# A fourth split slot at each stage's start, and four jobs side by side at three feed-forward starts

## The reference, cut to what matters

```python
def swiglu(x, w_gu, w_down):
    gate, up = jnp.split(x @ w_gu, 2, axis=-1)
    return (jax.nn.silu(gate) * up) @ w_down
...
    y = swiglu(rmsnorm(h, ffn1_pre_g[l]), ffn1_w_gu[l], ffn1_w_down[l])
    h = h + 0.5 * rmsnorm(y, ffn1_post_g[l])
    u = rmsnorm(h, mix_pre_g[l])
    proj = u @ w_in[l]
...
    h = h + rmsnorm(merged @ w_out[l], mix_post_g[l])
```

## Time and profile before

| | us |
|---|---|
| median of 3 runs (lowest, highest) | 3282.03 (3281.15, 3282.69) |
| the profiled execution, its own time | 3282.84 |
| its span | 3281.0 |
| PE busy | 3251.3 (99%) |
| DVE busy | 2377.1 (72%) |
| ACT busy | 1695.7 (52%) |
| POOL busy | 320.3 (10%) |
| boundary 1 to 2: first job of stage 2 starts at | 872.20 |
| boundary 2 to 3: first job of stage 3 starts at | 1216.07 |

### The profile page before, as it was taken

The page is one execution under the profiler, slowest core; times in us unless marked ns, Lnnn a source line. Parts: engine busy times, 40 slices in busy tenths (PEclk is TensorE's granted clock), DMA queues, the critical chain, the costliest instruction groups (busy, mean ns, idle before and its releaser), DMA issues.

```text
span 3281.0 us, 51592 instructions
## 1 busy us (share of the span) xinstructions
PE 3251.3 (99%) x20356; PEld 2902.2 (88%) x20356; DVE 2377.1 (72%) x4254; ACT 1695.7 (52%) x3071; POOL 320.3 (10%) x289
## 2 busy tenths in 40 slices
PE   9999999999999999999999999999999999999998
PEld 7999888888899998999888888899988888889998
DVE  7877764766697768777755766787868676658776
ACT  5555553645465545555553654564547374336553
POOL 1000110121010001000201121000000001201000
PEclk9999999999999999999999999999999999999999
DMA  4333433352233332333424263233332322322332
GB/s 143 109 105 121 125 81 87 84 153 89 85 99 102 113 99 90 110 103 116 125 68 125 54 151 103 68 110 107 109 100 88 93 77 71 103 96 97 101 112 84
DMA packets 118562, 332.80 MB, mean 101 GB/s; under 512 B 18984, under 2 KB 21800, under 8 KB 118320
## 3 DMA queue, kind: packets, MB, share of 16 engines
q1 hardware_dynamic: 106352, 308.40, 30.1%
q0 software_dynamic: 11680, 20.56, 3.2%
q10 hardware_dynamic: 288, 0.52, 0.0%
HBM read 306.23 MB, written 4.21 MB: 95 GB/s over the span
## 4 chain that ended last, share of the span: by engine, by line
PE 91%; DVE 6%; ACT 1%; DMA 1%; issue 1%; SPq 0%; POOL 0%; DVEq 0%; ACTq 0%
PE PS L838 89%; PE PS L1242 2%; DVE acc L1969 1%; DVE wl L1940 1%; DVE h L2024 1%; DVE tmp L2021 1%; DVE ul L1977 1%; DMA raw<-in_win 0%; ACT wh L1361 0%; DVE stk L2433 0%; DMA tmp<-tmp 0%; ACT tmp L1361 0%; SPq L3034 0%; ACT stk L1361 0%; DVE lru L2766 0%
## 5 line engine op out<-in xcount | busy, mean ns | idle before, releaser
L1940 DVE TENSOR_TENSOR wl<-raw,wh 128x1024 fp32r<-128x1024 f32 (+2 forms) x615 | 632.8, 1032 | 253.2 <-ACT wh L1361 247.4
L1361 ACT ACTIVATE wh<-raw 128x1024 fp32r<-128x1024 f32 (+2 forms) x619 | 535.0, 870 | 353.7 <-PE PS L838 331.8
L838 PE MATMUL PS<-bh,wh 128*128 128x256 f32 x2520 | 696.2, 276 | 0.0
L838 PE MATMUL PS<-bh,wl 128*128 128x256 f32 x2520 | 696.2, 276 | 0.0
L838 PE MATMUL PS<-bl,wh 128*128 128x256 f32 x2520 | 695.9, 276 | 0.0
L838 PE MATMUL PS<-uh,wh 128*128 128x512 f32 (+2 forms) x1368 | 525.6, 384 | 7.7 <-DVE stkf L2568 2.7
L838 PE MATMUL PS<-ul,wh 128*128 128x512 f32 (+2 forms) x1368 | 517.7, 378 | 0.0
L838 PE MATMUL PS<-uh,wl 128*128 128x512 f32 (+2 forms) x1368 | 517.5, 378 | 0.0
L838 PEld LDWEIGHTS PS<-bh,wh 128*128 128x128 f32 x2520 | 473.1, 188 | 0.6
L838 PEld LDWEIGHTS PS<-bh,wl 128*128 128x128 f32 x2520 | 473.0, 188 | 0.6
L838 PEld LDWEIGHTS PS<-bl,wh 128*128 128x128 f32 x2520 | 473.1, 188 | 0.0
(11 more groups left out here) (280 smaller groups left out, 5819.7 us busy)
## 6 DMA issues: line engine op xcount, KB each, us to landing
raw<-in_gu SPq DMA_DIRECT2D x218, 512.0 KB, 3.3
raw<-in_win SPq DMA_DIRECT2D x139, 512.0 KB, 3.5
raw<-in_dn SPq DMA_DIRECT2D x80, 320.0 KB, 2.9
raw<-in_dn SPq DMA_DIRECT2D x40, 512.0 KB, 3.6
raw<-in_wbr SPq DMA_DIRECT2D x72, 256.0 KB, 2.7
raw<-in_wout SPq DMA_DIRECT2D x24, 512.0 KB, 3.2
raw<-in_dn SPq DMA_DIRECT2D x40, 256.0 KB, 2.7
raw<-in_wv SPq DMA_DIRECT2D x20, 512.0 KB, 3.4
```

What stands on the lines that cost most here:

```text
L838: return e.matmul(out, lhs, rhs, start=start, stop=stop, skip_group_check=True)
L1361: return e.activation(out, in_, f, scale=scale, **more)
L1940: tt(lo, src, hi, SUB).then_inc(*S.lo.up(("lo", c)))
```

## The change

There are four opener slots a stage instead of three; `oh` moves to a lower place in the same area so that both hold four. The fourth job's cut p0+3 is now split with the other openers, ahead of the held tiles, on ACT and on DVE. With the slot free, cuts p0+4 to p0+7 wait for the cuts eight before. In the feed-forwards v = 2, 3 and 5 `group_halves` takes four jobs, so each k of a half is 12 matmuls of 256 columns; `after` is p0+4 and `more` is p0+5, `sums_pre` comes behind 6 matmuls of `after` and `spread_pre` behind 18. In the mixers v = 1, 4 and 6 three jobs stay side by side, and p0+3 is still `after`. In `mixer_2` (v = 6) two memsets move, since the fourth slot's neighbours now lie on their tiles.

```diff
-        oh = sb("oh", [P, 3, 1088], F32R, where["X"] + 57600)
-        ol = sb("ol", [P, 3, 1088], F32R, where["X"] + 57600 + 3 * 4352)
+        oh = sb("oh", [P, 4, 1088], F32R, where["X"] + 32768)
+        ol = sb("ol", [P, 4, 1088], F32R, where["X"] + 57600)
...
-        OPENERS = {first_of(v) + i: i for v in range(1, 7) for i in range(3)}
+        OPENERS = {first_of(v) + i: i for v in range(1, 7) for i in range(4)}
...
+                at = (1, 3) if len(jobs) == 4 else (3, 5)
                 n = 0
-                for _ in dense(after, v, "u"):
-                    n += 1
-                    if n == 3:
-                        sums_pre(v)
-                n = 0
-                for _ in dense(more, v, "u"):
-                    n += 1
-                    if n == 1:
-                        spread_pre(v)
+                for job in (after, more):
+                    for _ in dense(job, v, "u"):
+                        n += 1
+                        if n == at[0]:
+                            sums_pre(v)
+                        elif n == at[1]:
+                            spread_pre(v)
 
             def ffn(v):
                 order = [JOBS[a, v, f] for f in range(PLAIN) for a in ("gate", "up")]
-                begin(v, order[:3], order[3], order[4])
-                for job in order[5:]:
+                n = 4 if 0 < v < 7 else 3
+                begin(v, order[:n], order[n], order[n + 1])
+                for job in order[n + 2:]:
                     run(job, v)
...
-                ahead(p0 + 2)
+                ahead(p0 + 3)
                 act(small[:, 48:49], eps, ACT.Sqrt)
                 for job in held:
                     last(job, 0)
...
-                ahead(p0 + 2)
+                ahead(p0 + 3)
                 for job in held:
                     if not mixed:
                         add_part(job, 0)
...
             def mixer_2(v):
-                E.wait_ge(S.mm, "job", ("dn", 5, 7), 1)
-                e.memset(V[:, 0, :], 0.0)
-                e.memset(PT[:, 0, :], 0.0).then_inc(*S.dv.up(("zero",)))
                 rstd(v)
...
                 evacuate(JOBS["g", v, 0, 0], v)
+                e.memset(V[:, 0, :], 0.0)
+                e.memset(PT[:, 0, :], 0.0).then_inc(*S.dv.up(("zero",)))
                 stack(q)
```

More of the change, by code:

```diff
@@ L545, in split_of @@
             if c in OPENERS:
-                return oh[:, OPENERS[c], 16 + a:16 + z], ol[:, OPENERS[c], 16 + a:16 + z]
+                o = 16 if OPENERS[c] < 3 or [v for v in (2, 3, 5) if c == first_of(v) + 3] else 0
+                return oh[:, OPENERS[c], o + a:o + z], ol[:, OPENERS[c], o + a:o + z]
             o = 16 if c in HALVED else 0
```

## The result

The changed kernel takes **3301.04 us** (median of 6 runs, 3298.57 to 3306.23) against 3282.43 of the kernel before (6 runs beside it, 3281.15 to 3284.04): ratio 1.006 [1.005, 1.007], 18.6 us slower. The forecast was 3285.5, its range 3280.0 to 3289.5. The profiled execution took 3302.35 us with a span of 3300.5, 19.5 more than the span of before.

What follows compares the result with a forecast made beforehand. PE, busy 99% of the span, was taken as the bound. Feed-forwards +4.9 and mixers -1.4 gave +3.5 us on the profiled 3282.84; adjusted to the median, the forecast was 3285.5, range 3280.0 to 3289.5.

Steps and rivals of the forecast that it cites:

- wait on the cut, net: Before the fifth job in stages 2, 3, 5: PE waits for cut p0+4, net loss 0.4, 0.7, 0.4 us.
- wait at g(3): At k = 3 of `beside` in stages 2, 3, 5: PE waits 1.1, 1.2, 1.1 us for DVE's fourth g.
- The gain on offer and the wait that takes its place: Feed-forwards: 2.0 us to win in stage 3, 2.2 in 2 and 5; instead stage 3 waits 2.7 on `wl`.
- With it the fifth job ends at 1242.8 + 7.26: Stage 3: fifth job starts when its cut is ready, 1242.8, and ends at 1250.1 against 1249.4 before, +0.7 us.
- The second debt: Feed-forwards: later `spread_pre` makes DVE's `rb` late, 3.4 us in stage 3; PE waits 1.1 to 1.2 at g(3).
- the whole lateness reaches PE: Rival, chance 0.15: a step behind g(3) lacks slack, so PE ends as late as DVE; +6.7 us, 3288.7.
- The mixers: Stages 1, 4, 6: earlier gathers give -0.75 us each in 1 and 4; memsets make stage 6 +0.1; sum -1.4.
- The moved split: Ahead of the held tiles: one more split fits DVE's idle time, 0 us; if cover fails a little, +1.2.
- the new place of the slots: New place of `oh`: priced at nothing because reads are the same; an effect would show as matmuls slower than 0.118.

Runs made afterwards that it cites:

- filler: Changed kernel plus 12 matmuls of 512 columns, results unused, on PE ahead of the fifth job in stages 2, 3 and 5; 3295.02 us.
- the late factor alone: Against the kernel with four opener slots but three jobs side by side everywhere: `spread_pre` 12 matmuls later in stages 2, 3 and 5; 3288.67 us.
- the slots alone: Changed kernel with three jobs side by side in all stages, keeping four opener slots and the early fourth split; 3277.97 us.

## Why the prediction was wrong, step by step

Account of the profiled executions, the feed-forwards' 19.35 us split by the marks:

| term, stages 2, 3, 5 | forecast | measured | from |
|---|---|---|---|
| wait on the cut, net | 0.4, 0.7, 0.4 | 0.7, 0.6, 0.7 | "parts" with filler less before |
| clock behind it | not in the sum | 4.3, 3.1, 1.6 | "parts" after less with filler |
| wait at g(3) | 1.1, 1.2, 1.1 | 1.2, 1.2, 1.2 | "parts" to "pairs", after less before |
| first pairs, hesitation and slow pace | not in the sum | 0.3, 2.1, 2.3 | "pairs" to the end, after less before |

- *The gain on offer and the wait that takes its place*: right. The wait was 3.2 instead of 2.7, since PE was done some 0.8 earlier in stage 3 and 0.6 in the others: in the second half (and in stage 3 in the first half too) the matmuls went at 0.1133, not at the 0.1178 that I took from the first half. The cut's time, which sets the end, was right to 0.1 us.
- *"With it the fifth job ends at 1242.8 + 7.26"*: this step failed. It carries durations from rows at 2.4 GHz over to the far side of a standstill that those rows didn't have. The runs put 1.2 GHz there, 9.0 us in three stages. It was the largest term of all, and the forecast had it at zero without saying so. All six runs of the changed kernel have a mean clock of 0.994 to 0.996 (the kernel before has 0.998 or 0.999 in all but two of the 73 runs taken beside the experiments), so it isn't a matter of one execution.
- *The second debt*: right in place and size, shown by itself with the late factor alone. But the sum let it end at g(3). The rival "the whole lateness reaches PE" named the weights and operands of the first pair as the next due step; their lateness cost PE only some 0.2 us of waiting, and through the pace 4.7 us. The place was right, the price came by another way.
- *The mixers*: a gain, 1.05 and 2.0 where 0.75 was forecast for each; with the slots alone 1.2 and 1.0. The memsets eat a microsecond of stage 6, as forecast; its loss of 1.4 is about what the clock's fall behind its wait costs (3.4 us at half the clock).
- *The moved split* and *the new place of the slots* at nothing: right; the slots alone are no slower in any stage, and nor are their matmuls.

With the two missing terms (9.0 and 4.7) the sum for the feed-forwards is 4.9 + 13.7 = 18.6; 19.35 was measured.

## What to carry to other kernels

A wait of TensorE is priced in two parts, its length and what the clock costs behind it: durations read at full clock hold only where the engine doesn't stand still first, and in a seam that must stand still even work that is thrown away can be cheaper than idling (here by 6 us). When a group is widened, what other engines do in answer to its inserted steps moves with it, so the gain comes only if the next operands are moved too, into time in which their engine idles earlier (here VectorE, behind the held tiles). A debt that ends in a slack of a tenth of a microsecond isn't paid: look at the next due step behind it, of every engine that PE waits for (here it was a copy of ScalarE's).

## What the runs showed of the hardware

- TensorE's clock went from 2.4 to 1.2 GHz behind standstills of 3.2 us (3 of 3) and 2.7 to 2.8 us (3 of 3), in four of six behind 1.8 us (one kernel 3 of 3, another 1 of 3), and in none of three behind 1.2 us, at the start of stages 2, 3 and 5 between dense matmuls. In stage 6, behind a wait for DVE's evacuation of 1.5 to 1.7 us, it fell in four of nine traces. One fall cost 1.6 to 4.3 us beside the wait, by how long it lasted (3.4 to 10.2 us), and that differs behind equal waits.
- Dense matmuls of 256 columns have two paces at the same granted clock, 0.1133 and 0.1178 us. A hesitation of 0.1 to 0.5 us at a product's start stood before each of the long slow stretches, and each went on to the end of its 256-column matmuls, 48 to 56 us later; but not each hesitation brought one (stage 2 after had it and stayed fast). What sets the pace stays open.
- Some executions fell by the clock in places that no edit touched (the mixers, the first 25 us). At one place late in the two mixers of stages 1 and 4 PE waits for DVE's `stkf`, for a time that differs between the traces: where it was 2.3 to 3.8 us (five times) the clock fell and the stage took 526.8 to 528.2 us, and where it was 1.7 or less it took 523.2 to 525.2 and the clock held. The single times of one kernel differ by 3 to 12 us.
